# One gather of 8 KB rows per token-expert pair, and groups of four behind it, in an expert layer

## The chip, the cores and the metric

The kernel runs on one core of a Trainium2 chip. The metric is the device time of one execution in microseconds (us), from three runs. The engines are named as in the profile: PE (TensorE), DVE (VectorE), ACT (ScalarE), POOL (GpSimd) and SP (SyncE); 16 DMA engines serve the core.

## The reference

Two transformer blocks on 256 tokens of width 1024, all in fp32. The first has two feed-forward layers around a mixer of gated linear attention and block attention; the second has a mixer of a gated delta rule and an mLSTM, cross-attention to 256 memory tokens, and last an expert layer and a norm. Only the expert layer is touched here:

```
def peer_ffn(h, wq, sub_keys, u_table, v_table):
    q = (hf @ wq).reshape(t, PEER_HEADS, 2, PEER_HALF)          # t = 256 tokens, 8 heads, 2 halves of 128
    sc = jnp.einsum('thpd,hpnd->thpn', q, sub_keys)
    top_v, top_i = lax.top_k(sc, PEER_TOPK)                     # 16 of 128 keys in each half
    cand = (top_v[:, :, 0, :, None] + top_v[:, :, 1, None, :]).reshape(t, PEER_HEADS, kk)
    best_v, best_pos = lax.top_k(cand, PEER_TOPK)               # 16 of 256 sums
    expert_id = jnp.take_along_axis(cand_id, best_pos, axis=-1)
    gate = jax.nn.softmax(best_v, axis=-1)
    ...                                                         # per block of 128 tokens:
    u = jnp.take(u_table, eb, axis=0)
    act = jax.nn.gelu(jnp.einsum('phkd,pd->phk', u, xb), approximate=False)
    wgt = gb * act
    return jnp.einsum('phk,phkd->pd', wgt, jnp.take(v_table, eb, axis=0))
```

Each token chooses 16 experts in each of 8 heads out of 16384, and for each choice one row of 1024 numbers (4 KB) is read from the key table `u` and one from the value table `v`.

## The kernel before

The 256 tokens are two row blocks `r` of 128, one token per partition. In the expert layer the unit of work is a pair (head `hh`, row block `r`, slot `s`): 8 x 2 x 16 = 256 units. For each the kernel does two indirect DMAs on POOL's queue (L2428): one brings for each partition the 4 KB row of its expert from `peer_u_2`, one that from `peer_v_2`. Both land in a ring of `NGAT` = 12 buffers of 4 KB per partition, in the order in which `peer_order()` names them. A buffer is free again, and POOL may issue the gather that is 12 later, after its key row's dot ("dot"), its value row's matmuls ("mm"), or, for 8 value rows at the end, its sum ("vsum").

- The dot (L1790, DVE) multiplies a key row with the normed tokens `xn` and sums 1024 products into one column of `dots`.
- When the 32 dots of a head are done, one gelu (L2303, ACT) and one multiply with the gates (L1798, DVE) give the 32 weights `wgt` of the head.
- For each value row ACT writes a diagonal matrix of 128 x 128 with the weights (L2310, two buffers), and PE multiplies it with the row in two halves of 512 columns (L1102), which add up in four PSUM banks over all heads. For 8 of the last 32 value rows DVE adds weight times row to `h` instead (L1809).

`peer_order()` is read by every engine, so each works in the same order: key rows of head `hh` alternate with value rows of head `hh - 1`. The steps of routing the next head are pieces of a generator `route(hh)` that lies between them: two weight tiles (split on ACT at L1835 and DVE at L1125, then 24 matmuls each on PE), the products with the sub keys (L1076), the copies to SBUF (L1844, L2275), the top 16 of each half and of the sums, the picking of the ids (L1680 to L1725, DVE), and exp and gates. The last step of the order is `last_norm`, which adds the PSUM banks to `h` (L1754), squares and sums on ACT (L2285), takes the power on POOL and writes the normed row block out. Weights come from SP's queue into `raw`, ahead of use.

Each engine runs its own stream in order. Waits are semaphores: `at(name, key)` is the count that the matching `up` or `land` reaches.

Of the kernel before, what the change touches and what calls it, by code (L numbers as in the profile page):

```python
# [20 lines left out]
NGAT = 12  # L21
LEAD = 8
# [146 lines left out]
BY_ROW = [(r, s) for r in range(2) for s in range(16)]  # L169
BY_SLOT = [(r, s) for s in range(16) for r in range(2)]  # L170


def peer_order():

    n = itertools.count()
    for _ in range(6):
        yield "route", 0
    yield ("rows",)  # L180
    for hh in range(8):
        sums = iter(BY_SLOT) if hh else iter(())
        routing = hh
        for _ in range(LEAD if hh > 1 else 2 * LEAD):
            for r, s in itertools.islice(sums, 1):
                yield "v", next(n), hh - 1, r, s
            yield "route", routing
        if hh:
            yield "drain", hh
            routing = hh + 1  # L190
        for k, (r, s) in enumerate(BY_SLOT if hh else BY_ROW):
            if hh == 0 and k == 8:
                yield "drain", 0
            yield "u", next(n), hh, r, s
            for r2, s2 in itertools.islice(sums, 1):
                yield "v", next(n), hh - 1, r2, s2
            if hh == 0 and k == 8:
                routing = 1
            if k % 2 and (hh or k % 8 == 7):
                yield "route", routing  # L200
        yield "act", hh
    for r, s in BY_ROW:
        yield "sum" if s % 4 == 1 else "v", next(n), 7, r, s
        if r and s == 15:
            yield "last", 0
    yield "last", 1


GATHERS = [g for g in peer_order() if g[0] in ("u", "v", "sum")]


# [7 lines left out]
def program(nc, D, out, stack, book):  # L219
# [102 lines left out]
    ffn_row, subk, iota16, gfin2 = mem(18368, 1024), mem(19392, 2048), mem(21440, 16), mem(21456, 1024)  # L322
    gbuf = [mem(6080 + 1024 * i, 1024) for i in range(NGAT)]
    xn = grid(mem(22480, 2048), 2)
    pq, scs, sc2 = mem(24528, 512), mem(25040, 512), mem(25552, 512)
    ptop = mem(26064, 64).rearrange("p (two r s) -> p two r s", two=2, r=2)
    cand, best, wk = mem(26128, 1024), mem(27152, 64), mem(27216, 1024)
    best3 = grid(best[:, 0:32], 2)
    ixf = mem(28240, 128)
    gates, dots, wgt = (mem(28368 + 256 * i, 256) for i in range(3))  # L330
    psm, pjunk = mem(29136, 8), uf
    diag = [mem(4800 + 128 * i, 128) for i in range(2)]
# [33 lines left out]
    def tensor_engine():  # L366
# [718 lines left out]
        def peer():  # L1085
            ready = norm("ffn", h)
            acc = [bank(("out", i)) for i in range(4)]
            gens = {hh: route(hh, ready) for hh in range(9)}
            n_mm = 0
            for what, *args in peer_order():  # L1090
                if what == "route":
                    next(gens[args[0]], None)
                elif what == "drain":
                    for _ in gens[args[0]]:
                        pass
                elif what == "v":
                    n, hh, r, s = args
                    first, last = hh == 0 and s == 0, hh == 7 and s == 15
                    t.wait_ge(*at("diag", n))
                    t.wait_ge(*at(f"gather{n % NGAT}", n))  # L1100
                    for c in range(2):
                        ins = t.matmul(acc[r * 2 + c], diag[n_mm % 2], gbuf[n % NGAT][:, c * 512:(c + 1) * 512],  # L1102
                                       start=first, stop=last)
                    ins.then_inc(*up("mm", n))
                    n_mm += 1
# [8 lines left out]
    def vector_engine():  # L1114
# [632 lines left out]
        def last_norm(r, last_mm):  # L1747
            st = psm
            for n in range(2):
                hv = h[:, r, n * 512:(n + 1) * 512]  # L1750
                if n == 0:
                    v.wait_ge(*at("mm", last_mm))
                    v.wait_ge(*at("vsum", sum_n[0]))
                v.tensor_tensor(hv, hv, spot["out", r * 2 + n], ALU.add).then_inc(*up("last", r, "h", n))  # L1754
            v.wait_ge(*at("last_sq", r, 1))
            settle(v, v.tensor_tensor(st[:, 2:3], st[:, 0:1], st[:, 1:2], ALU.add), "last", r, "sum")
            v.tensor_scalar(st[:, 3:4], st[:, 2:3], 1.0 / 1024, EPS, ALU.mult, ALU.add).then_inc(*up("last", r, "ms"))
            v.wait_ge(*at("last_rs", r))
            if r == 0:
                v.wait_ge(*at("gfin2"))  # L1760
            for n in range(2):
                c = slice(n * 512, (n + 1) * 512)
                v.scalar_tensor_tensor(h[:, r, c], h[:, r, c], st[:, 4:5], gfin2[:, c], ALU.mult,
                                       ALU.mult).then_inc(*up("last", r, "out", n))

        sum_n = [None]

        def peer():
            norm("ffn", vecs[:, V_FFN, :], None, ("vec",))
            gens = {hh: route(hh) for hh in range(9)}  # L1770
            last_mm, last_dot = {}, None
            for what, *args in peer_order():
# [11 lines left out]
                elif what == "u":  # L1784
                    n, hh, r, s = args
                    c = hh * 32 + r * 16 + s
                    v.wait_ge(*at(f"gather{n % NGAT}", n))
                    if last_dot is not None:
                        v.wait_ge(*at("dot", last_dot))
                    v.tensor_tensor_reduce(pjunk, gbuf[n % NGAT], xn[:, r, :], 1.0, 0.0, ALU.mult, ALU.add,  # L1790
                                           dots[:, c:c + 1]).then_inc(*up("dot", n))
                    last_dot = n
                elif what == "act":
                    hh = args[0]
                    c = slice(hh * 32, (hh + 1) * 32)
                    v.wait_ge(*at("gelu", hh))
                    v.wait_ge(*at("chosen", hh, 1 if hh == 0 else 0))
                    v.tensor_tensor(wgt[:, c], wgt[:, c], gates[:, c], ALU.mult).then_inc(*up("wgt", hh))  # L1798
                elif what == "v":
                    last_mm[args[2]] = args[0]  # L1800
                elif what == "sum":
                    n, hh, r, s = args
                    c = hh * 32 + r * 16 + s
                    v.wait_ge(*at(f"gather{n % NGAT}", n))
                    if sum_n[0] is None:
                        v.wait_ge(*at("wgt", hh))
                    else:
                        v.wait_ge(*at("vsum", sum_n[0]))
                    v.scalar_tensor_tensor(h[:, r, :], gbuf[n % NGAT], wgt[:, c:c + 1], h[:, r, :], ALU.mult,  # L1809
                                           ALU.add).then_inc(*up("vsum", n))  # L1810
                    sum_n[0] = n
                elif what == "last":
                    last_norm(args[0], last_mm[args[0]])
# [10 lines left out]
    def scalar_engine():  # L1824
# [455 lines left out]
        def last_norm(r):  # L2280
            for n in range(2):
                if r and n == 0:
                    a.wait_ge(*at("last", 0, "sum"))
                a.wait_ge(*at("last", r, "h", n))
                a.activation(pjunk[:, n * 512:(n + 1) * 512], h[:, r, n * 512:(n + 1) * 512], ACT.Square,  # L2285
                             accum_out=psm[:, n:n + 1]).then_inc(*up("last_sq", r, n))

        def peer():
            norm("ffn", vecs[:, V_FFN, :], None, ("vec",))
            gens = {hh: route(hh) for hh in range(9)}  # L2290
            made, last_dot = [], None
            for what, *args in peer_order():
# [5 lines left out]
                elif what == "u":  # L2298
                    last_dot = args[0]
                elif what == "act":  # L2300
                    c = slice(args[0] * 32, (args[0] + 1) * 32)
                    a.wait_ge(*at("dot", last_dot))
                    a.activation(wgt[:, c], dots[:, c], ACT.Gelu).then_inc(*up("gelu", args[0]))  # L2303
                elif what == "v":
                    n, hh, r, s = args
                    c = hh * 32 + r * 16 + s
                    a.wait_ge(*at("wgt", hh))
                    if len(made) > 1:
                        a.wait_ge(*at("mm", made[-2]))
                    a.activation(diag[len(made) % 2], ident, ACT.Copy, scale=wgt[:, c:c + 1]).then_inc(*up("diag", n))  # L2310
                    made.append(n)
                elif what == "last":
                    last_norm(args[0])
# [22 lines left out]
    def gpsimd_engine():  # L2336
# [85 lines left out]
        freed_by = {}  # L2422
        for what, n, hh, r, s in GATHERS:
            if s == 0:
                p.wait_ge(*at("ids", hh, r if hh == 0 else 0))
            if n >= NGAT:
                p.wait_ge(*at(*freed_by[n - NGAT]))
            p.indirect_dma_start(gbuf[n % NGAT], None, D["peer_u_2" if what == "u" else "peer_v_2"],  # L2428
                                 bass.IndirectOffsetOnAxis(ap=id3[:, r, hh * 16 + s:hh * 16 + s + 1], axis=0)
                                 ).then_inc(*land(f"gather{n % NGAT}", n))  # L2430
            freed_by[n] = {"u": "dot", "v": "mm", "sum": "vsum"}[what], n
# [85 lines left out]
def layout(x):  # L2517
# [8 lines left out]
    def gu(g, u):  # L2526
# [38 lines left out]
        "peer_u_2": x["peer_u_2"][0], "peer_v_2": x["peer_v_2"][0],  # L2565
# [18 lines left out]
```

## Time and profile before

| | |
|---|---|
| median of 3 runs | 1885.03 us (1880.17 to 1889.42) |
| profiled execution | 1885.56 us, span 1884.1 us |
| busy over the span | PE 79%, DVE 60%, ACT 32%, POOL 33% |
| mean granted PE clock | 0.914 of full speed |
| DMA | 463.14 MB, mean 246 GB/s; POOL's queue 276.07 MB, SP's 183.52 MB |
| expert layer | from about 1050 us; gathers from 1097.1 us |

The span runs from the first to the last instruction of the profiled execution. A busy share is that of the whole span, over stages with different limits. A granted clock of 1.00 is 2.4 GHz, 0.50 is 1.2 GHz.

### The profile page before, as it was taken

How to read it: one execution, taken by the hardware profiler on the slowest of the kernel's cores; microseconds unless marked ns; L12 is line 12 of the kernel's file. 1: busy time of each engine (PE TensorE's matmuls, PEld its weight loads, DVE VectorE, ACT ScalarE, POOL GpSimd, SP SyncE). 2: the span in 40 equal slices, each digit the busy share in tenths (PEclk: the TensorE clock that was granted, in tenths of full speed). 3: DMA queues.
4: the chain of work that ended last, by engine and by line, in shares of the span. 5: the costliest groups of instructions: out<-in, count | busy, mean ns of one | idle time of the engine just before them, and what ended most of it. 6: DMA issues, size and time to landing. Idle time of an engine off the chain costs nothing.

```text
span 1884.1 us, 21211 instructions
## 1 busy us (share of the span) xinstructions
PE 1487.9 (79%) x7766; PEld 1127.4 (60%) x7766; DVE 1131.4 (60%) x1927; ACT 599.9 (32%) x1059; POOL 616.6 (33%) x573
## 2 busy tenths in 40 slices
PE   3799989999899988889988824938586868585667
PEld 3689978888799978889977721414242424242223
DVE  5366665865655456685664488566575656565442
ACT  2244444353444346443444411212121212111112
POOL 0000010000100000111000056777777677767673
PEclk8899989999999998899999966969898989898988
DMA  9577756655555643323353368999999999999996
GB/s 345 142 237 257 239 199 223 224 180 179 190 188 179 197 161 105 97 81 99 101 168 135 101 259 312 371 352 356 383 331 361 331 378 342 356 351 369 346 368 240
DMA packets 128633, 463.14 MB, mean 246 GB/s; under 512 B 15537, under 2 KB 15826, under 8 KB 128402
## 3 DMA queue, kind: packets, MB, share of 16 engines
q0 software_dynamic: 76672, 276.07, 40.0%
q1 hardware_dynamic: 50688, 183.52, 29.2%
q10 hardware_dynamic: 1170, 2.18, 0.3%
q8 instruction: 63, 1.03, 0.2%
q14 instruction: 40, 0.33, 0.0%
HBM read 459.62 MB, written 2.10 MB: 245 GB/s over the span
## 4 chain that ended last, share of the span: by engine, by line
PE 59%; DVE 13%; POOL 10%; issue 7%; DMA 7%; ACT 3%; another core or an unknown queue 1%; SPq 0%; ACTq 0%; DVEq 0%; POOLq 0%
PE ps L1102 14%; POOL Ft L2428 9%; PE ps L430 7%; PE ps L431 7%; PE ps L432 7%; DMA Ft<-peer_v,ids 3%; DVE Ft L1790 3%; PE ps L474 2%; PE ps L476 2%; PE ps L475 2%; PE ps L550 2%; PE ps L551 2%; PE ps L552 2%; PE ps L413 2%; DMA raw<-ff_dn 2%
## 5 line engine op out<-in xcount | busy, mean ns | idle before, releaser
L1102 PE MATMUL ps<-Ft 128*128 128x512 f32 x992 | 481.6, 633 | 221.3 <-issue 98.3
L1102 PEld LDWEIGHTS ps<-Ft 128*128 128x128 f32 x992 | 190.6, 201 | 499.4 <-issue 389.9
L1125 DVE TENSOR_TENSOR wlo<-raw,whi 128x1024 fp32r<-128x1024 f32 x268 | 324.2, 1235 | 180.4 <-ACT whi L1835 139.5
L1790 DVE CUSTOM_DVE_ANT_0 Ft<-Ft 128x1024 f32<-128x1024 f32 x256 | 313.8, 1226 | 168.6 <-DMA Ft<-peer_u,ids 143.3
L430 PE MATMUL ps<-uhi,whi 128*128 128x256 f32 x1280 | 374.5, 293 | 12.9 <-DVE wlo L1125 8.2
L431 PE MATMUL ps<-ulo,whi 128*128 128x256 f32 x1280 | 366.7, 286 | 0.0
L432 PE MATMUL ps<-uhi,wlo 128*128 128x256 f32 x1280 | 366.4, 286 | 0.0
L2428 POOL DMA_INDIRECT Ft<-peer_u,ids x256 | 280.9, 1097 | 125.7 <-issue 73.5
L2428 POOL DMA_INDIRECT Ft<-peer_v,ids x256 | 277.3, 1083 | 107.1 <-issue 65.6
L1835 ACT ACTIVATE whi<-raw 128x1024 fp32r<-128x1024 f32 x268 | 271.1, 1048 | 72.3 <-DMA raw<-ff_gu 29.0
L430 PEld LDWEIGHTS ps<-uhi,whi 128*128 128x128 f32 x1280 | 250.5, 196 | 19.0 <-issue 11.0
L431 PEld LDWEIGHTS ps<-ulo,whi 128*128 128x128 f32 x1280 | 250.5, 196 | 3.5 <-issue 1.9
L432 PEld LDWEIGHTS ps<-uhi,wlo 128*128 128x128 f32 x1280 | 250.0, 195 | 0.0
L2310 ACT ACTIVATE Ft<-Ft 128x128 f32<-128x128 f32 x248 | 96.3, 399 | 383.1 <-PE ps L1102 248.5
L2374 POOL TENSOR_TENSOR Ft<-Ft 128x512 f32<-128x512 f32 x6 | 8.6, 1440 | 400.4 <-DVE Ft L1245 400.3
L413 PE MATMUL ps<-Ft 128*128 128x128 f32 x224 | 40.6, 365 | 65.0 <-DVE Ft L1182 65.0
L1137 DVE SCALAR_TENSOR_TENSOR Ft<-raw,Ft 128x1024 f32<-128x1024 f32 x63 | 81.1, 1287 | 5.2 <-DMA raw<-w_ada 3.7
L1278 DVE TENSOR_TENSOR Ft<-ps,Ft 128x256 f32<-128x256 f32 x44 | 18.6, 423 | 104.6 <-ACT Ft L1939 104.6
L2349 POOL TENSOR_TENSOR Ft<-Ft 128x4 f32<-128x4 f32 (+1 forms) x5 | 5.7, 1134 | 231.3 <-DVE Ft L1302 231.3
L413 PEld LDWEIGHTS ps<-Ft 128*128 128x128 f32 x224 | 39.3, 277 | 67.3 <-DVE Ft L1182 67.3
L550 PE MATMUL ps<-whi,mhi 128*128 128x512 f32 x176 | 70.5, 401 | 10.4 <-DVE wlo L1125 10.4
L2344 POOL TENSOR_TENSOR Ft<-Ft 128x2 f32<-128x2 f32 x8 | 5.7, 709 | 210.3 <-DVE Ft L1173 210.3
(360 smaller groups left out, 1882.1 us busy)
## 6 DMA issues: line engine op xcount, KB each, us to landing
raw<-ff_gu SPq DMA_DIRECT2D x88, 512.0 KB, 4.8
raw<-w_ada SPq DMA_DIRECT2D x72, 512.0 KB, 4.9
raw<-ff_dn SPq DMA_DIRECT2D x44, 512.0 KB, 4.8
raw<-w_in SPq DMA_DIRECT2D x32, 512.0 KB, 3.6
raw<-w_in_s SPq DMA_DIRECT2D x28, 512.0 KB, 4.4
raw<-w_out SPq DMA_DIRECT2D x16, 512.0 KB, 4.3
raw<-peer_wq SPq DMA_DIRECT2D x16, 512.0 KB, 4.6
raw<-w_in_m SPq DMA_DIRECT2D x12, 512.0 KB, 4.3
```

The lines of the kernel that those rows point to most:

```text
L413: ins = t.matmul(o[:, k * 256 + r * 128:k * 256 + r * 128 + 128], src[:, r, (2 * q + k) * 128:(2 * q + k) * 128 + 128], dgr[:, r, :], star ...
L430: t.matmul(o, hi[:, c], x[0][:, i], start=(k == 0), stop=False)
L431: t.matmul(o, hi[:, c], x[1][:, i], start=False, stop=False)
L432: return t.matmul(o, lo[:, c], x[0][:, i], start=False, stop=(k == 7))
L550: t.matmul(acc[n, r], m[0][:, c], a, start=(f == 0), stop=False)
L1102: ins = t.matmul(acc[r * 2 + c], diag[n_mm % 2], gbuf[n % NGAT][:, c * 512:(c + 1) * 512], start=first, stop=last)
L1125: v.tensor_tensor(lo, raw_slot(j), hi.bitcast(F32), ALU.subtract).then_inc(*up("lo", j))
L1137: ins = v.scalar_tensor_tensor(acc, raw_slot(j), cact[:, k:k + 1], acc, ALU.mult, ALU.add)
L1790: v.tensor_tensor_reduce(pjunk, gbuf[n % NGAT], xn[:, r, :], 1.0, 0.0, ALU.mult, ALU.add, dots[:, c:c + 1]).then_inc(*up("dot", n))
L1835: a.activation(split_slot(j)[0], raw_slot(j), ACT.Copy).then_inc(*up("hi", j))
L2310: a.activation(diag[len(made) % 2], ident, ACT.Copy, scale=wgt[:, c:c + 1]).then_inc(*up("diag", n))
L2428: p.indirect_dma_start(gbuf[n % NGAT], None, D["peer_u_2" if what == "u" else "peer_v_2"], bass.IndirectOffsetOnAxis(ap=id3[:, r, hh * 16 ...
```

## The change

The two tables are laid side by side in memory as `peer_uv`, 16384 rows of 8 KB, so that one gather brings key and value row of a pair. The ring has 9 buffers of 8 KB per partition: 7 in the large SBUF tile and 2 in the two fp32r tiles `m`, whose gathers are issued with both sides as fp32r. Seven buffers lie where other data of the layer lay, which moves some small tiles; the gather of pair 6 waits for `xn` since its buffer covers the norm's row `ffn_row`.

The order is by pairs: a head's 16 pairs of row block 0, then those of block 1, in groups of four. After the last dot of a group comes its gelu; its gate multiply, its four diagonals and their matmuls stand behind the second dot of the next group. After every second pair lies one piece of routing of the next head. There are four diagonal buffers instead of two. All 256 value rows go through PE, none through DVE's sum. The last groups have 4, 2, 1 and 1 pairs, and the final norm of row block 0 is spread between the last pairs of block 1. A buffer is free after its pair's matmuls, and PE no longer waits for a gather, since the weights depend on it.

```
-NGAT = 12
-LEAD = 8
+NGAT = 9
+NDIAG = 4
...
+def peer_groups(hh):
+
+    last = (4, 4, 4, 2, 1, 1)
+    for r in range(2):
+        s = 0
+        for n in (last if hh == 7 and r == 1 else (4, 4, 4, 4)):
+            yield r, range(s, s + n)
+            s += n
...
     yield ("rows",)
+    yield "drain", 0
+    n, waiting = 0, []
     for hh in range(8):
...
+        k = 0
+        for r, slots in peer_groups(hh):
+            first = n
+            for s in slots:
+                yield "pair", n, hh, r, s
+                n, k = n + 1, k + 1
+                if waiting and (s == slots[0] + 1 or len(slots) == 1):
+                    yield from waiting
+                    waiting = []
+                if k % 2 == 0:
+                    yield "route", hh + 1
+                if hh == 7 and k in (22, 24, 30):
+                    yield "last", 0, (k - 22) // 2
+            yield "gelu", hh, r, slots
+            waiting = [("gate", hh, r, slots)] + [("v", first + s - slots[0], hh, r, s) for s in slots]
+        yield "drain", hh + 1
+    yield from waiting
+    for part in (0, 1, 4):
+        yield "last", 1, part
...
-    gbuf = [mem(6080 + 1024 * i, 1024) for i in range(NGAT)]
+    gbuf = [mem(6080 + 2048 * i, 2048) for i in range(NGAT - 2)] + [x[:, :].bitcast(F32) for x in m]
...
-                    t.wait_ge(*at(f"gather{n % NGAT}", n))
                     for c in range(2):
-                        ins = t.matmul(acc[r * 2 + c], diag[n_mm % 2], gbuf[n % NGAT][:, c * 512:(c + 1) * 512],
+                        ins = t.matmul(acc[r * 2 + c], diag[n % NDIAG],
+                                       gbuf[n % NGAT][:, 1024 + c * 512:1024 + (c + 1) * 512],
                                        start=first, stop=last)
...
+                elif what == "pair":
                     n, hh, r, s = args
                     c = hh * 32 + r * 16 + s
                     v.wait_ge(*at(f"gather{n % NGAT}", n))
...
+                    v.tensor_tensor_reduce(pjunk, gbuf[n % NGAT][:, 0:1024], xn[:, r, :], 1.0, 0.0, ALU.mult, ALU.add,
                                            dots[:, c:c + 1]).then_inc(*up("dot", n))
...
+                elif what == "gelu":
+                    hh, r, slots = args
+                    c = slice(hh * 32 + r * 16 + slots[0], hh * 32 + r * 16 + slots[-1] + 1)
+                    a.wait_ge(*at("dot", hh * 32 + r * 16 + slots[-1]))
+                    a.activation(wgt[:, c], dots[:, c], ACT.Gelu).then_inc(*up("gelu", hh, r, slots[0]))
...
+                    if n >= NDIAG:
+                        a.wait_ge(*at("mm", n - NDIAG))
+                    a.activation(diag[n % NDIAG], ident, ACT.Copy, scale=wgt[:, c:c + 1]).then_inc(*up("diag", n))
...
-        for what, n, hh, r, s in GATHERS:
+        for n, hh, r, s in PAIRS:
             if s == 0:
                 p.wait_ge(*at("ids", hh, r if hh == 0 else 0))
+            if n == 6:
+                p.wait_ge(*at("xn"))
             if n >= NGAT:
-                p.wait_ge(*at(*freed_by[n - NGAT]))
-            p.indirect_dma_start(gbuf[n % NGAT], None, D["peer_u_2" if what == "u" else "peer_v_2"],
+                p.wait_ge(*at("mm", n - NGAT))
+            dst, src = gbuf[n % NGAT], D["peer_uv"]
+            if n % NGAT >= NGAT - 2:
+                dst, src = m[n % NGAT - NGAT + 2][:, :], src.bitcast(F32R)
+            p.indirect_dma_start(dst, None, src,
...
-        "peer_u_2": x["peer_u_2"][0], "peer_v_2": x["peer_v_2"][0],
+        "peer_uv": np.concatenate([x["peer_u_2"][0], x["peer_v_2"][0]], 1),
```

## Rows read from the trace of the kernel before

**Rows 1.** The page's part 4, the chain that ended last, by engine and by line.

```profile
PE 59%; DVE 13%; POOL 10%; issue 7%; DMA 7%; ACT 3%; another core or an unknown queue 1%; SPq 0%; ACTq 0%; DVEq 0%; POOLq 0%
PE ps L1102 14%; POOL Ft L2428 9%; PE ps L430 7%; PE ps L431 7%; PE ps L432 7%; DMA Ft<-peer_v,ids 3%; DVE Ft L1790 3%; PE ps L474 2%; PE ps L476 2%; PE ps L475 2%; PE ps L550 2%; PE ps L551 2%; PE ps L552 2%; PE ps L413 2%; DMA raw<-ff_dn 2%
```

**Rows 2.** Busy time by stage: us, engines (count), granted clock, DMA share, GB/s.

```profile
core 0: us, PE busy (x) PEld busy (x) DVE busy (x) ACT busy (x) POOL busy (x), PEclk, DMA share, GB/s
1110.00:1120.00 10.00, 5.37 (x28) 5.19 (x28) 8.60 (x18) 2.95 (x6) 7.87 (x8) 0.67 1.02 413
1350.00:1355.00 5.00, 4.99 (x6) 2.19 (x7) 0.00 (x0) 0.65 (x2) 3.74 (x4) 0.50 1.01 390
1380.00:1415.00 35.00, 29.04 (x88) 13.61 (x87) 31.17 (x85) 7.67 (x19) 26.39 (x24) 1.00 0.96 353
1380.00:1470.00 90.00, 62.69 (x153) 26.82 (x152) 57.07 (x129) 18.20 (x43) 66.82 (x61) 0.91 0.96 354
1464.00:1467.80 3.80, 3.80 (x7) 1.50 (x6) 0.05 (x1) 1.35 (x2) 1.95 (x4) 0.55 0.88 293
```

**Rows 3.** Groups by line, from 1050 us to the end.

```profile
L1102 PE MATMUL ps<-Ft 128*128 128x512 f32 x992 | 481.6, 633 | 221.3 <-issue 98.3 <-ACT Ft L2310 68.2 <-DMA Ft<-peer_v,ids 54.6
...
L1790 DVE CUSTOM_DVE_ANT_0 Ft<-Ft 128x1024 f32<-128x1024 f32 x256 | 313.8, 1226 | 168.6 <-DMA Ft<-peer_u,ids 143.3 <-issue 5.5 <-DVE Ft L1790 0.5
...
L2428 POOL DMA_INDIRECT Ft<-peer_u,ids x256 | 280.9, 1097 | 125.7 <-issue 73.5 <-DVE ids L1725 29.3 <-DVE Ft L1790 11.3
...
L2428 POOL DMA_INDIRECT Ft<-peer_v,ids x256 | 277.3, 1083 | 107.1 <-issue 65.6 <-PE ps L1102 31.7 <-remote 9.8
...
L2303 ACT ACT_TABLE_LOAD x7 | 9.0, 1283 | 0.1
...
L2303 ACT ACTIVATE Ft<-Ft 128x32 f32<-128x32 f32 x8 | 1.8, 229 | 123.1 <-DVE Ft L1790 92.8 <-issue 30.4
```

**Rows 4.** Timeline of POOL: start us, us, what, idle before it.

```profile
1097.11 1.07 POOL L2428 DMA_INDIRECT Ft<-peer_u,ids  x1 [24.18 <-DVE ids L1725]
...
1117.59 1.07 POOL L2428 DMA_INDIRECT Ft<-peer_u,ids  x1 [0.30 <-issue]
...
1118.97 1.07 POOL L2428 DMA_INDIRECT Ft<-peer_u,ids  x1 [0.31 <-issue]
...
1165.52 0.93 POOL L2428 DMA_INDIRECT Ft<-peer_v,ids  x1 [1.37 <-PE ps L1102]
...
1167.24 0.94 POOL L2428 DMA_INDIRECT Ft<-peer_v,ids  x1 [0.78 <-PE ps L1102]
...
1175.04 0.94 POOL L2428 DMA_INDIRECT Ft<-peer_u,ids  x1 [5.14 <-DVE ids L1725]
```

**Rows 5.** Timeline of DVE, and last the line of the gate multiply.

```profile
1111.13 1.22 DVE L1790 CUSTOM_DVE_ANT_0 Ft<-Ft 128x1024 f32<-128x1024 f32 x1
...
1180.48 1.22 DVE L1790 CUSTOM_DVE_ANT_0 Ft<-Ft 128x1024 f32<-128x1024 f32 x1 [4.50 <-DMA Ft<-peer_u,ids]
...
1412.92 0.18 DVE L1704 TENSOR_SCALAR posu<-posu 128x32 uint32<-128x32 uint32 x1
...
1416.06 1.22 DVE L1790 CUSTOM_DVE_ANT_0 Ft<-Ft 128x1024 f32<-128x1024 f32 x1
...
1877.48 1.28 DVE L1754 TENSOR_TENSOR Ft<-Ft,ps 128x512 f32<-128x512 f32 x2
...
L1798 DVE TENSOR_TENSOR Ft<-Ft x8: 191/192/193, 1158.5 to 1822.8; 128x32 f32<-128x32 f32 x8
```

**Rows 6.** Timeline of ACT, the diagonal of one value row.

```profile
1163.04 0.40 ACT L2310 ACTIVATE Ft<-Ft 128x128 f32<-128x128 f32 x1 [3.64 <-PE ps L1102]
```

**Rows 7.** Timeline of PE: first and last matmul of a weight tile; values after a gap.

```profile
1087.49 0.36 PE L430 MATMUL ps<-uhi,whi 128*128 128x256 f32 x1
...
1090.32 0.28 PE L432 MATMUL ps<-uhi,wlo 128*128 128x256 f32 x1
...
1463.41 7.11 PE L1102 MATMUL ps<-Ft 128*128 128x512 f32 x12 [3.18 <-ACT Ft L2310]
```

## What I expect of the time

> **What bounds the kernel now.** I read first the chain that ended last, then busy time by stage, then groups by line in the expert layer, then timelines of POOL, DVE, ACT and PE. The chain gives the expert layer's value matmuls (L1102) and its gather issues (L2428) the largest shares of any lines [rows 1]. The layer runs from the first gather at 1097.1 us [rows 4] to the end at 1884.1: 787 us, of which one head takes 94.9 us (the gate multiply of a head starts at 1158.5 for the first and 1822.8 for the eighth, [rows 5]: 664.3 / 7). Only this stage is touched.
>
> It moves 512 gathers of 512 KB, 268.4 MB, and 14 weight tiles of 512 KB, 7.3 MB. In steady state the DMA engines show a share of 0.96 and 354 GB/s, but with gathers queued ahead and no buffer missing they reached 413 GB/s [rows 2]. So the transfers are near their bound, not on it. The resource that is full is POOL: in 90 us it was busy 66.8 us with 61 issues [rows 2], and consecutive issues stand 0.30 us apart even when nothing is waited for (1117.59 + 1.07 to 1118.97) [rows 4]; 66.8 + 61 x 0.30 = 85.1 of 90 us. DVE, PE and ACT were busy 57, 63 and 18 of those 90 [rows 2]. POOL's issues alone make 512 x (1.09 + 0.30) = 712 of the 787 us [rows 3, 4]; the rest is waits of the ring where routing or the matmuls lag.
>
> **The change part by part.**
>
> *Issues.* 256 instead of 512: 256 x 1.39 = 356 us of POOL. I take an issue of 8 KB rows at the old duration, since it also describes 128 rows; at twice that (2.14 + 0.30) POOL would have 625 us, still under what follows. POOL stops being the bound.
>
> *Transfers.* The bytes stay. One gather is 1.049 MB, at 413 GB/s 2.54 us; four 10.2 us. No row shows an indirect gather of 8 KB rows, so its rate is bounded: 354 GB/s (2.96 us) if it stays at the steady rate, 413 or a little more if longer rows save something. I take 413 while there is a queue.
>
> *The ring.* This is the new term. A buffer held 4 KB and a key row was free after its dot; now each of 9 buffers keeps both rows until its value matmul, which is sent out only after the group of four is done and two dots of the next group have run. Follow the buffer of a group's first pair. Its successor, four gathers later in the same place of the next group, is issued this long after the landing that releases it: dot 1.23, gate multiply 0.19 [rows 3, 5], hand-over 0.05, and from the start of the diagonal's ACT write to the next POOL issue 2.48 us (1163.04 to 1165.52) [rows 4, 6]: 3.95 us. From issue to landing an isolated 512 KB gather took 1175.04 to 1180.48, 5.44 us [rows 4, 5]; the second half adds 1.27 at 413 GB/s, 6.7 us. So four gathers need 3.95 + 6.7 = 10.65 us if latency decides, 10.2 if the transfers do. I take 10.5. Three gathers (7.6 us) are in flight over those 3.95 us, so DMA engines hardly run dry.
>
> *PE.* Two halves by two passes per pair: 1.72 us per pair at the high clock (POOL's issues released by them stand at 1165.52 and 1167.24) [rows 4], 6.9 us per group, which leaves PE idle for 3.6 of 10.5 us. After 3.2 us without work (to 1463.41) [rows 7] the granted clock was 0.55 in the next 3.8 us, near the lower level of 1.2 GHz [rows 2]; at 0.50 six of these matmuls took 4.99 us [rows 2], 3.3 us per pair against 1.72. If the burst begins there, the loop gets 1.6 us longer. From 1380 to 1415 us, with PE busy 29 of 35 us, it stayed at 2.4 GHz [rows 2]. I take it for one group in five: 0.3 us. The group's period is then 10.8 us. The Trainium skill, "TensorE: Matmul & The Clock Gate", Part 1, has the array throttled by default and released by activity; the trace agrees with the direction, and by that rule every burst after such a gap would begin slow, which is the second rival.
>
> *Routing beside it.* Once a head, PE has two weight tiles (24 matmuls, 1087.49 to 1090.60, 3.1 us each [rows 7]) between value groups, and ACT's gelu stands behind the copies that wait for them. Values 0.5 + 6.9, tile 3.1, copy and key product 0.9, tile 3.1: the next values start 14.5 us after a gate instead of 11.3, 3.2 late. The two tiles' own transfer is 2.5 us, a third of it exposed. 4 us for each of 7 heads = 28; bounds 0 and 5.7. DVE has 57 us of work per head [rows 2], seven more gate multiplies of 0.19; its dearest routing piece is 3.1 us (1412.92 to 1416.06) [rows 5], with two dots 5.9 against 5.4 us for two pairs, made good at the next cheaper piece. ACT: 66 gelus of 0.23 instead of 8, 13 us over the layer, and the table loads (1.28 each [rows 3]) stay two a head, since all gelus of a head but those next to its exp share a table. All this lies under the 10.8 us.
>
> *Start.* The first dot is unchanged at 1111.1 [rows 5], since head 0's routing precedes it in both. The ninth gather lands at 1097.1 + 6.7 + 8 x 2.54 = 1124. The first group frees nothing before: four dots and a tile's low half (5.5 + 1.2) to 1117.8; ACT behind tile and copies to about 1123, table load and gelu 1.5, gate and diagonal 0.7, first values at the low clock 3.3: issue of the tenth gather at 1129. DMA idles some 6 us. Bounds 1126 and 1133.
>
> *End.* Row block 0 is normalised before; block 1 has last groups of 2, 1, 1. From the last landing: dot 1.2, gelu 0.2, gate 0.2, diagonal to matmul end 2.4 = 4.1; from the last sum (1877.48 [rows 5]) to the end 6.6.
>
> *Sum.* 1129 + 61.5 groups (246 gathers / 4) x 10.8 = 664, + 28, + landing 6.2 (between 5.8 and 6.7), + 4.1 + 6.6 = 1838. The profiled execution's time is 1.5 us over its span and 0.5 over the median of the runs: 1840 us, 2.4% less than now.
>
> **The rivals.**
>
> *Better than the ring allows* (0.14). Group period 9.8 to 10.2, routing hidden: 1127 + 61.5 x 10 + 6 + 4 + 7 = 1759 to 1790 us with up to 28 of routing. For it: 413 GB/s were seen; against it: the 6.7 us of latency.
>
> *The low clock in each burst* (0.20), the rival of the other sign. One mechanism: PE idles 3.6 us before each group of values, the group starts at 1.2 GHz, the first buffer comes free 1.6 to 1.8 us later, and this again lengthens the idle time. Period 12.3: 1129 + 756 + 28 + 17 = 1930, 1932 us. It decides from a period of 11.5 (1884.1 - 1129 - 28 - 17 = 710; / 61.5), which is the low clock in somewhat over half of the groups. For it: the rows at 1463 us; against it: while routing tiles run PE has no gap, and a PE that is late has no gap either and gets its clock back.
>
> *The memory is the limit already* (0.05). If 358 GB/s were a ceiling for the core, 275.7 MB would take 770 us: 1097 + 1.5 + 770 + 6 idle at the start + 11 = 1886, no change. The window at 413 GB/s [rows 2] speaks against it. The Trainium skill, "DMA: Bandwidth & Descriptors", Specifications, gives about 358 GB/s as the memory's limit for one core; this trace shows more than that.
>
> *The two buffers in the fp32r tiles are slower* (0.03). 57 of the 256 gathers are written as fp32r; nothing in this trace shows such a gather. If each took twice 2.54 us, and that exposed, + 145 us: about 1985. The Trainium skill, same page, SWDGE vs HWDGE vs iDMA, says that an fp32r destination always casts; it gives no price.
>
> **How the numbers follow.** The likeliest case has 0.58, and 1840 us with a range of its own of 1800 to 1875 (period 10.2 to 11.4). The range 1780 to 1910 leaves out half of the better case, some two fifths of the low-clock case, and the fp32r case, 0.07 + 0.08 + 0.03. Half a per cent, about what a measurement tells from no change here, is 9 us. Faster: 0.58 + 0.14 + 0.02 of the low-clock case = 0.74; same: 0.05 + 0.02 = 0.07; slower: 0.16 + 0.03 = 0.19.
>
> **What would show it.** POOL's busy time in a 90 us stretch should fall from 67 to about 36 us; DVE's dots should be 2.7 us apart on average, and wait for gathers, not POOL's issue; ACT should wait for landings and gelu groups of four; a head should take 90 us (the ids' casts, L1725 before); DMA some 385 GB/s. POOL's issues should wait for the value matmuls. The granted clock should be at 2.4 GHz in four groups of five. Wrong if gathers of 8 KB rows land later than 7.5 us after issue, if the clock falls before most groups, or if DVE has no idle time left between dots.

## The result and the profile after

The changed kernel took 1908.53 us in the median of 4 runs (1907.27 to 1921.45), the kernel before 1887.18 beside it: a ratio of 1.0135, with an interval of 1.0083 to 1.0187. It is 1.3% slower, where 2.4% faster was forecast; the time itself lies just inside the upper end of the range given. The profiled execution has a span of 1906.3 us.

The page's part 4 of the changed kernel, the chain that ended last by engine and by line, against [rows 1]:

```profile
PE 56%; DMA 22%; DVE 10%; issue 7%; ACT 4%; POOL 1%; SPq 0%; ACTq 0%; DVEq 0%; POOLq 0%
DMA Ft<-peer_uv,ids 16%; PE ps L1102 12%; PE ps L432 7%; PE ps L433 7%; PE ps L434 7%; PE ps L476 2%; PE ps L477 2%; PE ps L478 2%; DMA mhi<-peer_uv,ids 2%; DMA mlo<-peer_uv,ids 2%; PE ps L552 2%; PE ps L553 2%; PE ps L554 2%; PE ps L415 2%; DMA raw<-ff_dn 2%
```

The gather issues (9% before, now L2415) are gone from the head of the list, as forecast. Landings of gathers have taken their place: 20% of the span (16 + 2 + 2) where the value gathers had 3%.

Busy time by stage of the changed kernel (columns as in [rows 2]):

```profile
core 0: us, PE busy (x) PEld busy (x) DVE busy (x) ACT busy (x) POOL busy (x), PEclk, DMA share, GB/s
1141.00:1145.20 4.20, 4.09 (x5) 1.85 (x6) 3.88 (x12) 0.94 (x4) 0.03 (x1) 0.50 0.95 382
1189.00:1196.20 7.20, 7.09 (x16) 2.96 (x16) 2.78 (x5) 1.14 (x5) 3.47 (x3) 1.00 0.95 378
1290.00:1380.00 90.00, 64.65 (x173) 30.70 (x172) 55.99 (x134) 16.86 (x48) 32.48 (x29) 0.92 0.93 354
1380.00:1470.00 90.00, 65.32 (x167) 30.89 (x166) 51.41 (x127) 15.89 (x47) 28.38 (x29) 0.87 0.84 322
```

In the same 90 us as before, 1380 to 1470, POOL is busy 28 us instead of 67, and nothing else is full: DVE 51, PE 65, the DMA share 0.84 with 322 GB/s instead of 0.96 with 354. In five stretches of 90 us from 1200 us on, the share lies between 0.84 and 0.93 and the rate between 322 and 354 GB/s. Every resource has slack, the DMA engines the least, and the layer isn't shorter. That points to a loop in which each step waits for the one before it.

Groups by line in the layer, of the changed kernel:

```profile
L1788 DVE CUSTOM_DVE_ANT_0 Ft<-Ft 128x1024 f32<-128x1024 f32 x200 | 245.1, 1226 | 189.7 <-DMA Ft<-peer_uv,ids 178.2 <-issue 5.2 <-DVE idu L1684 0.6
...
L2415 POOL DMA_INDIRECT Ft<-peer_uv,ids x200 | 220.2, 1101 | 411.8 <-PE ps L1102 372.7 <-DVE ids L1725 24.2 <-issue 14.9
...
L1788 DVE CUSTOM_DVE_ANT_0 Ft<-mlo,Ft 128x1024 f32<-128x1024 f32 x28 | 34.3, 1226 | 30.7 <-DMA mlo<-peer_uv,ids 29.7
...
L1788 DVE CUSTOM_DVE_ANT_0 Ft<-mhi,Ft 128x1024 f32<-128x1024 f32 x28 | 34.3, 1226 | 27.9 <-DMA mhi<-peer_uv,ids 27.1
```

POOL's issue of a gather takes 1.10 us on average for 8 KB rows and 1.10 and 1.08 for 4 KB rows [rows 3]: the first part of the prediction holds. Its 200 issues into the large tile waited 372.7 us for value matmuls. The dots waited for landings. Those from the two fp32r tiles waited 1.1 and 1.0 us each (30.7 / 28, 27.9 / 28), those from the large tile 0.95 (189.7 / 200): no sign that these gathers are slower.

The chain in order of time, four of its gathers that follow each other (start, us from issue to landing); the pieces between them are left out:

```profile
1255.77 7.37 DMA mlo<-peer_uv,ids
1268.18 6.42 DMA Ft<-peer_uv,ids
1280.18 6.25 DMA mhi<-peer_uv,ids
1290.51 7.86 DMA Ft<-peer_uv,ids
```

Each is the gather of the second pair of a group, the first of the four that POOL may issue when the value matmuls of a group free their buffers. From one issue to the next stand 12.4, 12.0 and 10.3 us, and the larger part of each is the landing: 7.4, 6.4, 6.3. What remains, called the release from here on, is the way from the landing over dot, gate multiply, diagonal and matmuls to the next issue. It is shown here once in its slow and once in its fast form (timelines of DVE, ACT, PE and POOL; start, us, what, idle before it):

```profile
1139.31 1.23 DVE L1788 CUSTOM_DVE_ANT_0 Ft<-Ft 128x1024 f32<-128x1024 f32 x1 [1.11 <-DMA Ft<-peer_uv,ids]
...
1140.66 1.28 ACT L2294 ACTIVATE Ft<-Ft 128x128 f32<-128x128 f32 x4 [5.73 <-DVE Ft L1795]
...
1141.11 3.78 PE L1102 MATMUL ps<-mlo,Ft 128*128 128x512 f32 x4 [4.93 <-ACT Ft L2294]
...
1145.17 1.88 POOL L2415 DMA_INDIRECT mlo<-peer_uv,ids  x1 [7.29 <-PE ps L1102]
...
1187.32 1.22 DVE L1788 CUSTOM_DVE_ANT_0 Ft<-Ft 128x1024 f32<-128x1024 f32 x1 [2.81 <-DMA Ft<-peer_uv,ids]
...
1188.66 1.28 ACT L2294 ACTIVATE Ft<-Ft 128x128 f32<-128x128 f32 x4 [6.37 <-DVE Ft L1795]
...
1189.11 1.98 PE L1102 MATMUL ps<-Ft 128*128 128x512 f32 x4 [2.96 <-ACT Ft L2294]
...
1191.37 1.59 POOL L2415 DMA_INDIRECT Ft<-peer_uv,ids  x1 [3.50 <-PE ps L1102]
```

Landing at 1139.31, dot, gate multiply, diagonal at 1140.66, first matmul at 1141.11, next issue at 1145.17: 5.9 us. The second time 1187.32, 1188.66, 1189.11, 1191.37: 4.05 us, where 3.95 was worked out. The difference is the matmuls: the windows above show 0.50 from 1141.0 to 1145.2 and 1.00 from 1189.0. Before the first PE had stood idle for 4.9 us, before the second for 3.0.

Read in this way over 60 groups of the trace (landing of the second pair of each group, taken from the start of its dot, and the POOL issue four gathers later), the release takes 5.01 us on average, never under 4.05, and more than 4.8 in 58% of the groups. The granted clock at the first four value matmuls of a group agrees: it was low in 59%. The landing takes 6.85 us, if five groups beside the routing are left out. In those the dot starts 13.1 us after the issue, which makes 0.5 us more per group. That isn't a late landing: in changed_again, a second run of the same kernel, whose trace records every landing, these five gathers landed after 5.5 to 8.1 us, and their dots started after 12.7 to 14.1. DVE, which works in order, stood at a routing step before the dot, as here for the gather issued at 1204.82:

```profile
1215.21 1.23 DVE L1125 TENSOR_TENSOR wlo<-raw,whi 128x1024 fp32r<-128x1024 f32 x1 [8.79 <-ACT whi L1819]
```

The sum, 12.4 us, is the measured pace: 246 gathers between the issues at 1121.7 and 1878.0 us make 61.5 groups of 12.3.

Landing and release aren't independent of each other. After a release at the high clock (under 4.4 us, 19 groups) the next landing took 7.9 us on average; after a slow one (over 5.2 us, 24 groups) it took 6.3. The sum is 12.0 us in both cases, and 12.1 and 12.0 in changed_again. An early release issues its gather while earlier ones are still being moved; a late one finds the DMA engines nearly idle. In the microsecond that begins 0.5 us after the issue, the DMA share was 0.18 on average for the 17 landings of under 6 us, and 0.97 for the 25 of over 7. Two stretches of the trace show it, one at the issue at 1246.15, which landed after 5.5 us, and one behind the issue at 1255.77, which took 7.4:

```profile
1246.00:1247.00 1.00, 1.00 (x3) 0.38 (x2) 0.86 (x3) 0.00 (x0) 0.85 (x1) 1.00 0.16 66
1257.00:1258.00 1.00, 1.00 (x4) 0.47 (x3) 0.34 (x3) 0.00 (x0) 0.51 (x1) 1.00 1.04 418
```

It goes round: behind a landing of over 7 us PE has been idle for long, and 24 of 25 such releases were slow; behind one of under 6.6 us, 8 of 23. So the groups often swing between some 10 us (short landing, fast release) and 13.6 (long landing, slow release).

### The profile page after: what moved, and what is told of

Its sections match the earlier page's. It is cut to its first block, busy times and chain, and to the rows that moved or that the text cites. A ratio compares the mean times of both kernels' runs of the same rounds, so it can differ in the third digit from the quotient of the medians.

```text
span 1906.3 us, 20739 instructions
## 1 busy us (share of the span) xinstructions
PE 1532.4 (80%) x7798; PEld 1148.7 (60%) x7798; DVE 1122.4 (59%) x1977; ACT 599.2 (31%) x1127; POOL 342.6 (18%) x317
## 3 DMA queue, kind: packets, MB, share of 16 engines
q8 instruction: 62, 1.02, 0.2%
## 4 chain that ended last, share of the span: by engine, by line
PE 56%; DMA 22%; DVE 10%; issue 7%; ACT 4%; POOL 1%; SPq 0%; ACTq 0%; DVEq 0%; POOLq 0%
DMA Ft<-peer_uv,ids 16%; PE ps L1102 12%; PE ps L432 7%; PE ps L433 7%; PE ps L434 7%; PE ps L476 2%; PE ps L477 2%; PE ps L478 2%; DMA mhi<-peer_uv,ids 2%; DMA mlo<-peer_uv,ids 2%; PE ps L552 2%; PE ps L553 2%; PE ps L554 2%; PE ps L415 2%; DMA raw<-ff_dn 2%
## 5 line engine op out<-in xcount | busy, mean ns | idle before, releaser
L1102 PE MATMUL ps<-Ft 128*128 128x512 f32 x800 | 414.5, 673 | 162.0 <-ACT Ft L2294 162.0
L1102 PEld LDWEIGHTS ps<-Ft 128*128 128x128 f32 x800 | 168.0, 216 | 396.8 <-issue 202.1
L1788 DVE CUSTOM_DVE_ANT_0 Ft<-Ft 128x1024 f32<-128x1024 f32 x200 | 245.1, 1226 | 189.7 <-DMA Ft<-peer_uv,ids 178.2
L2415 POOL DMA_INDIRECT Ft<-peer_uv,ids x200 | 220.2, 1101 | 411.8 <-PE ps L1102 372.7
L432 PEld LDWEIGHTS ps<-uhi,whi 128*128 128x128 f32 x1280 | 250.1, 195 | 19.8 <-issue 10.9
L2294 ACT ACTIVATE Ft<-Ft 128x128 f32<-128x128 f32 x256 | 82.1, 390 | 323.3 <-DVE Ft L1795 316.9
L1102 PE MATMUL ps<-mlo,Ft 128*128 128x512 f32 x112 | 62.8, 689 | 26.4 <-ACT Ft L2294 26.4
L1102 PE MATMUL ps<-mhi,Ft 128*128 128x512 f32 x112 | 62.1, 683 | 24.2 <-ACT Ft L2294 24.2
L415 PEld LDWEIGHTS ps<-Ft 128*128 128x128 f32 x224 | 37.6, 266 | 67.4 <-DVE Ft L1182 67.4
L2286 ACT ACTIVATE Ft<-Ft 128x4 f32<-128x4 f32 (+1 forms) x66 | 13.4, 203 | 205.0 <-DVE Ft L1788 205.0
```

Source lines behind the costliest of these rows:

```text
L415: ins = t.matmul(o[:, k * 256 + r * 128:k * 256 + r * 128 + 128], src[:, r, (2 * q + k) * 128:(2 * q + k) * 128 + 128], dgr[:, r, :], star ...
L432: t.matmul(o, hi[:, c], x[0][:, i], start=(k == 0), stop=False)
L1102: ins = t.matmul(acc[r * 2 + c], diag[n % NDIAG], gbuf[n % NGAT][:, 1024 + c * 512:1024 + (c + 1) * 512], start=first, stop=last)
L1788: v.tensor_tensor_reduce(pjunk, gbuf[n % NGAT][:, 0:1024], xn[:, r, :], 1.0, 0.0, ALU.mult, ALU.add, dots[:, c:c + 1]).then_inc(*up("dot", n))
L2294: a.activation(diag[n % NDIAG], ident, ACT.Copy, scale=wgt[:, c:c + 1]).then_inc(*up("diag", n))
L2415: p.indirect_dma_start(dst, None, src, bass.IndirectOffsetOnAxis(ap=id3[:, r, hh * 16 + s:hh * 16 + s + 1], axis=0)).then_inc(*land(f"gath ...
```

## The experiments

Ratios are to the kernel before, measured beside each kernel on the same chip. It took 1885 us on the chip of gate1, ring8, warm and split4k and 1850 to 1851 us on the three chips of the others; the changed kernel took 1908 us beside a kernel before of 1887, and 1916 in changed_again. Kernels that ran on different chips are compared by their ratios and by the pace of a group in the trace. Three readings are put against each other: the ring theory (the loop landing, dot, gate, diagonal, matmul, issue sets the pace), the clock theory (PE's slow starts do) and the rate theory (8 KB rows are moved slowly).

**gate1: the release one dot earlier.**

```
-                if waiting and (s == slots[0] + 1 or len(slots) == 1):
+                if waiting:
```

> The gate multiply and the four value rows of a group go out behind the first dot of the next group, not the second. Ring theory (the loop landing, dot, gate, diagonal, matmul, issue, landing sets a group's 12.1 us): the landing that releases a buffer is one gather earlier, and each release then serves a landing two groups later, so the loop no longer closes within one group; the transfers decide, 10.2 to 10.8 us a group, 1815 to 1840 us. Clock theory (the low clock at the start of the bursts makes the loss): the gaps of PE stay, 1890 to 1905 us. Rate theory (gathers of 8 KB rows deliver no more than 350 GB/s): 1900 to 1910 us, no change.

1816.24 us, ratio 0.9598 (0.9538 to 0.9658). One line turns 1.3% slower into 4.0% faster, in the range of the ring theory. Its window by stage:

```profile
1380.00:1470.00 90.00, 70.21 (x185) 32.99 (x184) 58.79 (x140) 18.21 (x52) 42.58 (x33) 0.92 0.97 380
```

DMA share 0.97 and 380 GB/s; the pace is 10.8 us a group. The release still took 4.8 us on average, with the clock low at the start of 34% of the bursts. Clock and rate theories had both put it at 1890 us or more and fall as main causes.

**ring8: one buffer less.**

```
-NGAT = 9
+NGAT = 8
```

> One buffer less, 8 for 9, nothing else. Ring theory: the gather that the next release waits for is issued by the second value row instead of the first, 1.7 us later in each of 61.5 groups: + 105 us, 2000 to 2020 us. Clock theory: PE's gap gets 1.7 us longer, the same order. Rate theory: no change while a queue exists, under + 20 us.

2100.31 us, ratio 1.1118 (1.1065 to 1.1171): 192 us more than the changed kernel, 3.1 us a group, nearly twice what the ring theory had expected. POOL's timeline shows two releases:

```profile
1307.03 1.16 POOL L2415 DMA_INDIRECT Ft<-peer_uv,ids  x1 [8.56 <-PE ps L1102]
...
1308.81 0.94 POOL L2415 DMA_INDIRECT Ft<-peer_uv,ids  x1 [0.62 <-PE ps L1102]
...
1322.50 1.08 POOL L2415 DMA_INDIRECT Ft<-peer_uv,ids  x1 [9.31 <-PE ps L1102]
...
1325.08 0.94 POOL L2415 DMA_INDIRECT Ft<-peer_uv,ids  x1 [1.50 <-PE ps L1102]
```

The gather that the next release waits for is the second of each, 2.58 us behind the first at 1325.08, 1.78 at 1308.81 (2.3 on average over the trace). The rest is the release itself, 5.95 us with not one group under 5.4: PE stood idle for 5.3 us before a burst instead of 3.4, and 60 of 61 bursts start at the low clock. 2.3 + 0.94 = 3.2, for the 3.1 measured. The window by stage from 1300 to 1360:

```profile
1300.00:1360.00 60.00, 39.19 (x76) 16.99 (x77) 20.57 (x40) 9.93 (x26) 16.54 (x16) 0.77 0.76 278
```

**warm: PE kept busy in its gap.**

```
+NWARM = 3
...
+                elif what == "gate":
+                    for _ in range(NWARM):
+                        t.matmul(spare, ident, subk[:, 0:512], start=True, stop=True)
```

> Three extra matmuls of 128x512 per group on a spare PSUM bank, ahead of the wait for the diagonal, so that PE is busy 2.6 us longer of the gap; their result isn't used. Clock theory: the bursts start at 2.4 GHz, 0.8 us or more less a group, 1850 to 1870 us. Ring theory: only the part of the loop that ran at 1.2 GHz is won back, about a third of 1.7 us in each group at most, 1870 to 1900 us; where PE is late behind routing tiles the extra matmuls cost 2.6 us, 8 times, + 20.

1900.72 us, ratio 1.0076 (1.0047 to 1.0105). Slow releases fall from 58% to 22% of the groups and the mean release from 5.01 to 4.53 us. The landings get longer by part of that (6.98 for 6.85), and a group takes 11.94 instead of 12.30: 22 us over the layer. At the end the extra matmuls stand before the last values: 34.9 us from the last issue to the end, 28.3 in the changed kernel. What is left in the time, 0.6% by the ratios, isn't clear of the noise; it fits neither the clock theory's 1850 to 1870 us nor quite the ring theory's 1870 to 1900. The clock is a term of the loop with its own price, 0.36 us a group here, where gate1 wins 1.5.

**ring8_warm: the same in the longer loop.** The diff is that of ring8 and warm together.

> ring8 with the three extra matmuls of warm. ring8 took 3.1 us more a group than the changed kernel where the later issue explains 1.7 to 2; its trace shows the low clock in nearly all bursts (issue 5.96 us after the landing on average, 5.03 in the changed kernel, 4.05 at the high clock). If the clock is the rest: 1 to 1.9 us less a group, 1985 to 2040 us. If the clock only goes along with the wait: 2080 to 2105 us.

2079.71 us, ratio 1.1221 (1.1166 to 1.1277). By the total this is the second case of what was expected: nothing like 1 us a group comes back. Three matmuls fill part of the longer gap (2.9 us are left of 5.3), and 73% of the releases stay slow. Mean release 5.46 instead of 5.95, pace 14.97 instead of 15.43: what the release gains, the group gains nearly whole.

**gate1_ring8: the two opposite edits together.**

> The release behind the first dot of the next group, as in gate1, and 8 buffers. The gather that the next release waits for is then again the first that this release issues, as in the changed kernel. Ring theory: the loop is the same and so is the time, 1895 to 1920 us. If the place of the gate multiply is worth its 90 us for another reason (DVE or ACT less in each other's way), it keeps most of that with a buffer less: 1830 to 1860 us.

1911.17 us, ratio 1.0313 (1.0257 to 1.0369); the changed kernel, where the kernel before took the same 1850 us, had 1.0351 (1.0305 to 1.0396). The pace is 12.3 us, that of the changed kernel. An earlier release with a buffer less gives the same loop (the first gather of a release is the one that the next waits for) and the same time, so that it is not the place of the gate multiply on DVE or ACT that makes gate1 fast.

**grp2: groups of two, release where the change has it.**

```
-    last = (4, 4, 4, 2, 1, 1)
+    last = (2,) * 7 + (1, 1)
...
-        for n in (last if hh == 7 and r == 1 else (4, 4, 4, 4)):
+        for n in (last if hh == 7 and r == 1 else (2,) * 8):
```

> Groups of two, the release behind the second dot of the next group as in the changed kernel, 9 buffers. Ring theory: a release issues gathers that the third release after it waits for, so that three groups of two share one loop of 11 to 12 us, under 4 us each where the transfers need 5.1: the transfers decide, 1800 to 1830 us. If the cost lay in the number of gelus, gate multiplies and waits, twice as many of them would make it slower than 1908 us.

1793.07 us, ratio 0.9695 (0.9649 to 0.9741). Twice as many gelus, gate multiplies and waits, and 6.4% less than the 1916.08 us of the changed kernel; 7 us under the range that the ring theory gave. Four gathers take 10.5 us.

**grp2_gate1: both.**

> Groups of two and the release behind the first dot of the next one. Ring theory: the loop had no share left in either alone, so both together give nothing in steady state; fewer value rows are left at the end (5 us): 1795 to 1825 us. If the loop still cost something in gate1, 20 us or more below it.

1773.91 us, ratio 0.9586 (0.9542 to 0.963), 19 us under grp2 and 21 under the range expected: the second case, in which the loop had still cost something. Four gathers take 10.1 us instead of 10.5. The end, for which 5 us were expected, gained nothing (26.5 us from the last issue, 24.9 in grp2). Its window:

```profile
1380.00:1470.00 90.00, 74.31 (x201) 33.55 (x200) 67.19 (x172) 22.39 (x66) 41.24 (x36) 0.98 1.02 411
```

411 GB/s at a DMA share of 1.02: here the transfers are the bound, and the pace is that of free8k below, where the loop is gone (10.1). This is the fastest full version: 4.1% under the kernel before, 7.4% under the changed one.

**split4k and grp2_gate1_split4k: what the longer row is worth.**

```
+            for i, table in enumerate(("peer_u_2", "peer_v_2")):
...
+                p.indirect_dma_start(dst[:, i * 1024:(i + 1) * 1024], None, src,
```

> The two tables apart again and two gathers of 4 KB rows per pair into the halves of the same buffer, everything else as changed. Ring theory: the second issue is 1.24 us behind the first, so that a pair lands 1.2 us later in each group's loop: + 50 to + 75 us, 1960 to 1985 us. Rate theory (8 KB rows are slow): the rate is that of before, 1885 us or less.

1976.09 us, ratio 1.0473 (1.043 to 1.0517), 68 us more than the changed kernel. The pace is 13.2 us. Of the 0.9 more, the wait from the pair's first issue to its dot takes 0.35 (7.2 us) and the release 0.5 (5.5 us, slow in 89% of the groups): the longer loop again brings its slow starts with it.

> grp2_gate1 (ratio 0.959 to before) with two gathers of 4 KB rows per pair instead of one of 8 KB. Where the loop no longer binds, only POOL's issues and the transfers' rate are left: free4k was 2% slower than free8k (0.979 against 0.960). If that is all that the row's length is worth: ratio 0.975 to 0.99, still under before. If a later landing still counts in this order, as in split4k (1.047 against 1.013): 0.99 to 1.01.

1841.85 us, ratio 0.9942 (0.9912 to 0.9973), 3.7% over grp2_gate1. The whole interval lies above the first of the two ranges and at the lower end of the second, so the row's length is worth more in this order than the 2% between free4k and free8k. Its window:

```profile
1380.00:1470.00 90.00, 69.09 (x182) 31.23 (x181) 58.31 (x145) 20.50 (x59) 70.80 (x64) 0.94 1.00 367
```

64 issues and 70.8 us of POOL; with 0.30 us between issues 90.0 of 90. With the ring in order, POOL is the bound that the prediction saw in the kernel before, and the 8 KB row takes it away. The joined row was the good part of the change. Whether the rest of the 3.7% is a later landing, as the expectation had it, wasn't tested.

**free8k and free4k: the gathers by themselves.**

```
-                p.wait_ge(*at("mm", n - NGAT))
+                p.wait_ge(*at(f"gather{n % NGAT}", n - NGAT))
...
```

> Dots and value matmuls read fixed tiles and wait for no gather; a gather waits only for the landing nine gathers before. The same 256 gathers of 8 KB rows then run without the loop (the output isn't the layer's). If their rate is the bound: 256 x 2.9 to 3.0 us, the layer as long as now. If the loop is: 400 to 420 GB/s, 256 x 2.5 us = 645 us, the whole 1775 to 1800 us, if DVE's order (about 70 us a head) doesn't hold the ids back.

1776.46 us, ratio 0.9599 (0.9512 to 0.9686). The window of free8k:

```profile
1380.00:1470.00 90.00, 73.22 (x204) 34.88 (x203) 69.55 (x167) 20.34 (x58) 40.89 (x36) 0.98 1.03 421
```

421 GB/s in each of five such windows. Gathers of 8 KB rows can be done at 2.5 us each; the change got one per 3.1 us.

> The same with two gathers of 4 KB rows per pair from the separate tables. POOL's 512 issues of 1.24 to 1.38 us make 635 to 705 us. If the length of a row matters to the transfers, this is slower than with 8 KB rows by that alone: equal if the DMA engines bind both at 413 GB/s, 30 to 60 us slower if POOL binds here.

1812.57 us, ratio 0.9794 (0.9717 to 0.9871). The window of free4k:

```profile
1380.00:1470.00 90.00, 73.15 (x204) 34.79 (x203) 69.51 (x170) 20.12 (x57) 70.10 (x66) 0.98 1.03 385
```

POOL makes 66 issues in 90 us, 70.1 + 19.8 us: full. 385 GB/s here, 402 at most in the five windows. It is 2.0% over free8k, two runs of each.

The DMA share is 1.03 in both kernels and can't tell which of them the transfers bind. The time from issue to landing can (free8k above, free4k below):

```profile
DMA to landing us min/median/max: 5.8/22.1/26.0
...
DMA to landing us min/median/max: 4.3/6.5/9.7
```

With 8 KB rows the gathers queue until the ring is full, and POOL waits for landings. With 4 KB rows they land 6.5 us after issue though eighteen may be in flight, and POOL never waits for one for more than a moment (0.9 us in all): the transfers keep up, and POOL is the bound. The same holds for grp2_gate1 (12.3 us in the median) and grp2_gate1_split4k (6.2).

**changed_again.**

> The changed kernel once more, beside the next one on the same chip: 1.3% over the kernel before, as its first measurement (ratio 1.0135).

1916.08 us, ratio 1.0351 (1.0305 to 1.0396), not the 1.0135 expected. The pace is 12.3 us again. The ratio is larger mainly because the kernel before took 1850.49 us on this chip. The change loses both times, but how much isn't settled: 1.3% in the one, 3.5% in the other.

## Why the prediction was wrong

*What bounds the kernel before* held: POOL's issues. In grp2_gate1_split4k and free4k, with two gathers of 4 KB rows a pair, POOL is full again as soon as the ring lets it be.

*Issues and transfers* held. An issue takes 1.10 us whatever the row; the rate without the loop is 421 GB/s, a little over the 413 taken.

*The ring* was the right mechanism, with the right gather and the right engines in it. Its threshold held too: from 11.5 us a group on, routing left out, the change loses, and 11.8 were measured. The step that failed is the period of a group, 10.8 us (11.25 with routing), for which 12.3 was measured. From the tenth issue to the last that is 756 us for the 692 of the sum. These terms were too small:

- *The low clock*, "I take it for one group in five: 0.3 us": 58% of the groups, and 0.96 us between the mean release and one at the high clock. This is 0.66 us a group, 41 us, the largest. The price of a slow burst was about right: 1.6 us were taken, and the release took 5.6 us with the low clock and 4.2 without. Its frequency was not. PE's gap had been taken as 3.6 us before every burst. It was 3.4 on average, but unequal: 4.0 us (2.0 to 6.1) before the bursts that began slow and 2.4 (up to 3.5) before the others.
- *The landing*, 6.55 us within "I take 10.5": 6.85. The value had been taken between a bound from latency, 6.7, and one from the transfers. Neither describes it: the mean is made of 17 landings of 5.3 to 5.9 us, most on nearly idle DMA engines, 25 of 7.1 to 9.2 behind other gathers, and 13 between. The row behind the 6.7 wasn't an isolated gather either: POOL issued four more at 1176.28, 1177.52, 1178.76 and 1180.00, before its dot at 1180.48. 0.3 us, 18 us.
- *Routing*: 0.52 us a group for 0.46; the release at the high clock 4.05 for 3.95. 10 us together.

These make 1.1 us, and 1.05 was measured over all 61.5 groups. They are shares of the two means, not what each would give back if it were mended: after a fast release the next landing was 1.6 us longer, and warm won 0.36 us a group from 0.48 of release. The forecast of 10.8 stood only 0.7 us under its own threshold of 11.5 (both without routing), which the low clock's term nearly fills. The chance of 0.19 for slower was too small for that distance. Two of the prediction's own signs of being wrong came: gathers landed more than 7.5 us after issue (8.5 us in the median in changed_again), and the clock was low at the start of most groups.

*The start* was forecast at 1129, measured 1121.7: 7 us early.

*The end*: 4.1 us from the last landing to the last sum were forecast. In the trace:

```profile
1878.00 0.94 POOL L2415 DMA_INDIRECT Ft<-peer_uv,ids  x1 [0.78 <-PE ps L1102]
...
1882.33 1.22 DVE L1788 CUSTOM_DVE_ANT_0 Ft<-Ft 128x1024 f32<-128x1024 f32 x1 [1.80 <-DMA Ft<-peer_uv,ids]
...
1884.13 5.14 PE L1102 MATMUL ps<-Ft 128*128 128x512 f32 x8 [4.68 <-ACT Ft L2294]
...
1892.54 7.03 PE L1102 MATMUL ps<-Ft 128*128 128x512 f32 x16
...
1899.61 1.28 DVE L1753 TENSOR_TENSOR Ft<-Ft,ps 128x512 f32<-128x512 f32 x2 [7.84 <-PE ps L1102]
```

The last issue stands at 1878.00 and the dot of pair 253 at 1882.33; only then go out the values of pairs 248 to 251, and the remaining four stand behind them on PE. 32 matmuls from 1884.13, eight of them over 5.14 us at the low clock, end at 1899.6. The sum had counted one pair's matmuls behind the last landing, where the rule of the groups leaves eight pairs unsent. From the last issue to the end 28.3 us for 16.9: 11 us. 64 - 7 + 11 = 68, the distance between 1838 and the span of 1906.3.

*The rivals*: the low clock in each burst was the nearest. It named the price and the threshold, and gave 12.3 us as the period, but by a loop that was too fast otherwise and a clock that was too slow: 58% of the bursts, not all. warm shows that taking most of the slow starts away leaves the kernel slower than before. The memory's limit as a rival fell with free8k: the 358 GB/s of the Trainium skill, "DMA: Bandwidth & Descriptors", Specifications, isn't the ceiling of a core alone here; 421 GB/s were held over 90 us. The fp32r rival fell by the dots' waits, and in changed_again these gathers landed after 8.1 and 8.3 us on average, the others after 8.3; there are 56 of them, not 57.

What stays open: what the fixed part of a landing is (5.3 to 5.9 us with the DMA engines nearly idle, where the transfer itself takes 2.5), and why the kernel before differs by 1.9% between sets of runs, which stood on different chips, and the changed kernel by 0.4. Of the change's other parts, the four diagonal buffers, all value rows on PE and the new end weren't tested by themselves.

## What to carry to other kernels

For a ring of n buffers, write down which landing releases a buffer and which issue of that release the next landing waits for. If this closes within one group of work, the period is the full latency of issue, landing and release, even though no engine is full; a release one item earlier makes two groups share it. By the same count one buffer more would do it too: that wasn't run, but a buffer less undid the earlier release exactly (gate1_ring8). Here the one line was worth 5.3% (1.0135 against 0.9598), four times the loss.

Where a term depends on the period (the clock after a gap, the queue that a gather finds), work it out again at the period that comes out, and then compare with the threshold. A forecast that lies within one such term of its threshold hasn't decided the sign.

A DMA share near 1 doesn't show that the transfers are the bound: look at whether the time from issue to landing grows until the ring is full.

## What was not expected of the hardware

- Gathers of 8 KB rows ran at 421 GB/s on one core, of 4 KB rows at 383 to 402 (90 us windows), with POOL full in the second case; the DMA share was 1.02 to 1.05 in both.
- The kernel before took 1885 to 1887 us in two sets of runs and 1850 to 1851 in three others, on other chips, 1.9% apart, while the changed kernel took 1908 beside one of 1887 and 1916 beside one of 1850. No run shows why.
- With PE gaps that come back every 12 us, the clock was low at the start of 58% of the bursts: those had gaps of 2.0 to 6.1 us before them, the others of up to 3.5.
- A gather of 8 KB rows landed 5.3 to 5.9 us after issue where the DMA engines were mostly idle, and 7.1 to 9.2 us after it behind others.
